# Two of a unit's four weight blocks asked for ahead of a store instead of behind it, in the first half of an MLP

## The reference, cut to what matters

```python
h = layer_norm(ALPHA * x + mix, ln1_g, ln1_b)                    # h: 576 x 2048
f = jnp.einsum('btf,fd->btd',
      jnp.square(jax.nn.relu(jnp.einsum('btd,df->btf', h, w_mlp1))), w_mlp2)   # w_mlp1: 2048 x 8192
y = layer_norm(ALPHA * h + f, ln2_g, ln2_b)
```

## Time and profile before

| | |
|---|---|
| median of 3 runs | 2890.78 us (2887.44 to 2892.32) |
| the profiled execution | 2880.25 us, its span 2878.5 us |
| PE, DVE, ACT busy | 92%, 68%, 36% of the span |
| stores of the loop | 30, at 1334.5 to 2068.9 us |
| mean granted TensorE clock | 0.963 of full speed |

### The profile page before, as it was taken

How to read it: one execution, slowest core, us unless ns; L and a number is a source line. 1 busy time by engine, 2 the same in 40 slices (tenths; PEclk the granted TensorE clock), 3 DMA queues, 4 the chain that set the end, 5 groups by cost and what they waited for, 6 DMA issues and landing times.

```text
span 2878.5 us, 52028 instructions
## 1 busy us (share of the span) xinstructions
PE 2651.6 (92%) x20033; PEld 2507.7 (87%) x20033; DVE 1950.1 (68%) x3064; ACT 1047.5 (36%) x1311; POOL 52.1 (2%) x106
## 2 busy tenths in 40 slices
PE   8999999988888899959999999999979999999997
PEld 8999999975555589948898999898979999999995
DVE  5778722337753443388777777777768888888897
ACT  3111111126754431154444444444433333333334
POOL 0000000000001000000000000000000000000000
PEclk9999999999999889979999999999999999999998
DMA  8766533223044444314555555555596566555632
GB/s 250 225 222 229 156 74 87 75 101 139 0 162 186 181 138 137 120 67 133 159 156 174 164 169 168 161 149 174 169 325 210 170 217 186 184 186 174 196 109 75
DMA packets 470707, 457.36 MB, mean 159 GB/s; under 512 B 47740, under 2 KB 418644, under 8 KB 459830
## 3 DMA queue, kind: packets, MB, share of 16 engines
q1 hardware_dynamic: 465370, 389.02, 44.2%
q0 software_dynamic: 4608, 67.11, 6.2%
q10 hardware_dynamic: 652, 0.18, 0.0%
HBM read 367.70 MB, written 96.80 MB: 161 GB/s over the span
## 4 chain that ended last, share of the span: by engine, by line
PE 38%; DVE 14%; DMA 10%; issue 8%; SPq 4%; ACT 2%; DVEq 0%; POOL 0%; ACTq 0%; POOLq 0%
PE ps L2235 24%; DMA w_s<-in_w_mlp 8%; PE ps L1899 7%; SPq L526 4%; DVE w_sl L1537 4%; DMA sg<-in_cache_slc,idx 3%; PE ps L2041 2%; DVE w_s L1542 1%; DVE w_s L1548 1%; ACT w_sh L934 1%; PE ps L2152 1%; PE ps L2051 1%; PE ps L2117 1%; PE ps L2104 1%; DVE f_raw L1686 1%
## 5 line engine op out<-in xcount | busy, mean ns | idle before, releaser
L2235 PE MATMUL ps<-h_b,w_sh 128*128 128x288 f32 x3584 | 740.2, 303 | 89.5 <-DVE w_sl L1537 67.9
L934 ACT ACTIVATE w_sh<-w_s 128x1024 fp32r<-128x1024 f32 (+1 forms) x512 | 469.9, 947 | 798.4 <-PE ps L2235 387.2
L2235 PE MATMUL ps<-f_b,w_sh 128*128 128x288 f32 x3584 | 717.7, 296 | 17.1 <-DMA f_b<-f_scratch 10.3
L2235 PEld LDWEIGHTS ps<-h_b,w_sh 128*128 128x128 f32 x3584 | 591.0, 194 | 102.2 <-DVE w_sl L1537 78.9
L1537 DVE TENSOR_TENSOR w_sl<-w_s,w_sh 128x1024 fp32r<-128x1024 f32 (+1 forms) x512 | 551.5, 1087 | 107.0 <-ACT w_sh L934 106.7
L2235 PEld LDWEIGHTS ps<-f_b,w_sh 128*128 128x128 f32 x3584 | 577.2, 189 | 20.1 <-DMA f_b<-f_scratch 11.2
L2235 PE MATMUL ps<-h_b,w_sl 128*128 128x288 f32 x1792 | 537.5, 300 | 0.0
L2235 PE MATMUL ps<-f_b,w_sl 128*128 128x288 f32 x1792 | 528.7, 295 | 0.0
L2235 PEld LDWEIGHTS ps<-h_b,w_sl 128*128 128x128 f32 x1792 | 348.6, 195 | 0.0
L2235 PEld LDWEIGHTS ps<-f_b,w_sl 128*128 128x128 f32 x1792 | 340.5, 190 | 0.0
L738 ACT ACTIVATE w_hi<-w_raw 128x2048 fp32r<-128x2048 f32 x61 | 117.0, 1918 | 613.9 <-PE ps L1899 609.7
(11 more groups left out here) (272 smaller groups left out, 2656.8 us busy)
## 6 DMA issues: line engine op xcount, KB each, us to landing
w_s<-in_w_mlp SPq DMA_DIRECT2D x512, 256.0 KB, 4.0
f_scratch<-f_st SPq DMA_DIRECT2D x32, 2016.0 KB, 7.6
f_b<-f_scratch SPq DMA_DIRECT2D x56, 1152.0 KB, 8.1
w_raw<-in_w_in SPq DMA_DIRECT2D x90, 512.0 KB, 5.2
x_r<-x_scratch SPq DMA_DIRECT2D x16, 576.0 KB, 5.0
wb<-in_cache_win SPq DMA_DIRECT2D x8, 1024.0 KB, 10.0
w_raw<-in_w_out SPq DMA_DIRECT2D x64, 128.0 KB, 2.9
w_raw<-in_w_out SPq DMA_DIRECT2D x16, 512.0 KB, 4.3
```

Source lines behind the costliest of these rows:

```text
L934: nc.scalar.activation(w_sh[m][:, :, :], blocks, ACT.Copy).then_inc(z_h[m], 1)
L2235: last = nc.tensor.matmul(ps[:, bank, 0:TH], w[b][:, at_, cols], acts(k, x), start=(start and k == 0 and n == 0), stop=(stop and k == CK - ...
```

## The change

The loop asks for blocks 2 and 3 of unit 1 ahead of the store, and for blocks 0 and 1 behind it. The wait for `z_l[M4]`, which stood behind the store, moves ahead of it with the first two blocks.

```diff
-            def w_blocks(view, c, q, u):
-
-                for b in (2, 3, 0, 1):
+            def w_blocks(view, c, q, u, blocks=(2, 3, 0, 1)):
+
+                for b in blocks:
...
-            def up_load(q, h):
+            def up_load(q, h, blocks=(2, 3, 0, 1)):
 
                 sp.wait_ge(z_l[M4], 2 * q + h - 1)
-                w_blocks(w1_v, h, q, h)
+                w_blocks(w1_v, h, q, h, blocks)
...
             with sp.Fori(0, KP - 2) as i:
                 up_load(i + 2, 0)
+                up_load(i + 2, 1, (2, 3))
                 f_store(i)
-                up_load(i + 2, 1)
+                w_blocks(w1_v, 1, i + 2, 1, (0, 1))
```

## The result

The changed kernel takes 2902.32 us, the kernel before 2887.44 us over the runs that stood beside it (medians of 5 each). The ratio is 1.0058, with a 95% interval of 1.0036 to 1.0080: slower by 0.6%, some 17 us (the two medians differ by 14.9 us). The direction was forecast, and the time lies in the range; but the size was given as 36 us, twice what came.

What follows compares the result with a forecast made beforehand. The prediction took a ring of waits, with DVE waiting for the last weight block, as the bound; 0.61 + 0.4 + 0.2 = 1.2 us a pair, 30 times, is 36 us, so 2890.8 becomes 2927 us; 8 in 10: 2899 to 2945.

Steps and rivals of the forecast that it cites:

- The ring: In the loop, 10.7 us from `low_22` to landed blocks plus 14.6 us of DVE's queue make the whole 25.3 us pair.
- Early blocks buy nothing: At DVE's one wait for all four blocks, only the last block's landing counts; blocks 2 and 3 landing early gain nothing.
- The later start: At the head of the DMA group, nothing can be issued until `low_22` is done; costs 0.61 us a pair, nearly certain.
- The sum: Added cost on DVE's wait for blocks: 0.61 + 0.4 + 0.2 = 1.2 us a pair, between 0.61 and 1.74.
- the new climb: Blocks with nothing ahead begin late and slowly, 0.22 + 0.41 us at most; taken as 0.4 us a pair.
- the turn: Between the first two blocks and the store the DMA rate dips; taken as 0.2 us a pair, ends 0 and 0.5.
- only the start counts: Rival: slow first bytes and the change from loads to store hide; 0.3 to 0.9 us a pair, 2909 us; chance 0.17.
- the store runs faster with fewer blocks behind it: Rival: the store gives back up to 1.1 us a pair, so not slower, 2883 us; chance of faster 0.09.
- The clock: Rival: PE's longer idle time draws the low clock, a pair 2 us longer or more, 2951 us and up; chance 0.06.
- unit 0's blocks: Loads asked for after unit 0's `low_22`; they and DVE's use of them shift together, costing nothing.
- the tile f_st: Tile that the later-landing store frees for ACT; needed only in the next pair, with 6 us or more of cover.
- The forecast of 11.8 us: Sign in the changed trace: first block's issue to last one's landing takes 11.8 us in place of 10.6.

Runs made afterwards that it cites:

- two counters: Changed kernel's order, but `sum_1` waits only for blocks 2 and 3, and `sum_23` for blocks 0 and 1; ratio to the kernel before 0.9983.
- the store in last place: Against the kernel before, all four blocks of unit 1 are asked for ahead of the store; 2791.7 us, ratio 0.9659.
- the kernel in which the store waits: Order of the kernel before, store then all four blocks, but the store is held until `low_22` is done; ratio to the kernel before 1.0054.
- one ahead: Changed kernel's lines with block 2 ahead of the store and blocks 3, 0 and 1 behind it; ratio to the kernel before 1.0045.
- three ahead: Changed kernel's lines with blocks 2, 3 and 0 ahead of the store and block 1 behind it; ratio to the kernel before 1.0021.
- half of the blocks asked for late: Against the kernel before: store first, then blocks 2 and 3, then a wait before blocks 0 and 1; ratio 0.9995.

## Why the prediction came out as it did

*The ring.* Right, link by link. DVE's part stayed at 14.61 us on average, the pair grew by what DVE's wait for the last block grew by, 0.58 us, and two counters and the store in last place moved the time as the ring says.

*Early blocks buy nothing.* Right: 0.71 us came back only when `sum_1` got a counter of its own.

*The later start, 0.61 us.* Right: 0.60 us when done alone.

*The sum, 1.2 us a pair.* Wrong, and this is the step that failed: "The bytes ahead of it are the same", from which I let the store and the blocks keep their durations and added only costs. By the table the recorded durations came to 1.79 + 5.56 + 1.73 = 9.08 us of each engine, where the kernel in which the store waits has 6.11 + 3.86 = 9.97: 0.89 us less, 0.55 of it in the store and 0.34 in the loads, of which four in a row fall to 290 GB/s after the second and two in a row do not.

That isn't 0.89 us of time given back, because durations can overlap. The stretch itself, averaged over 29 pairs, shows the balance:

```
                 first issue to  first byte to  last byte to  sum
                 first byte      last byte      DVE's start   us
store waits      0.87            9.68           0.59          11.14
one ahead        1.04            9.38           0.55          10.97
changed kernel   1.04            9.66           0.42          11.12
three ahead      1.04            9.36           0.36          10.76
```

The durations of the kernel in which the store waits, 9.97 us, lie in 9.68 us, so some of them do overlap; the changed kernel's 9.08 us lie in 9.66 us. So the first bytes came 0.17 us later, where the sum had 0.22; the new climb and the turn were paid for inside the stretch, which kept its length because the store and the loads took less; and the wait behind the last byte, which the sum left out, became 0.17 us shorter, for a reason that is not shown. In place of the 0.4 + 0.2 us of the sum, these terms came to -0.02 us. How much the climb and the turn cost by themselves isn't shown, only that what was given back is as large. The dip that I feared between load and store didn't come.

*The rival "only the start counts"* gave the right number (0.3 to 0.9 us a pair, 18 us in the middle; measured 0.58 and 17), but not its reason: the climb was there and was outweighed, by a store and loads that took 0.89 us less of each engine. That the balance came out at zero is luck, as it did not with one or three blocks ahead. The formula with a fixed part and bytes over a rate ("DMA: Bandwidth & Descriptors", "Anatomy of one DMA", in the Trainium skill) gives that same 18 us, and by it the experiments with 0, 1, 2 and 3 ahead would all take 25.9 us; three ahead took 25.54, so it is right by chance here.

*The rival "the store runs faster with fewer blocks behind it"* had the right effect, though only in part the right reason: a store with fewer blocks behind it is shorter, but not because fewer issues are held up (half of the blocks asked for late), and loads ahead of it shorten it too. I talked myself out of it with one row. In the earlier trace rows a store with one load behind had the same ragged end as one with four, and I concluded that loads behind don't slow it. One load behind is enough: that store took 5.79 us, against 4.87 with none. The comparison needed a store with none behind, which the loop of before doesn't have. The size that I gave it, 1.1 us at most, is near what the last places gave: 6.10 against 4.82 to 4.93. One of the signs of being wrong was that the store's bytes run clearly faster than now, and it came: 5.56 us of each engine in place of 6.10.

*The clock* stayed near 0.96 (0.963 before, 0.960 after), *unit 0's blocks* and *the tile f_st* gave no wait, as costed. The forecast of 11.8 us from first issue to last landing came out as 1610.98 - 1600.01 = 10.97 us in the pair shown, and about 11.1 on average. PE's wait for DVE's low parts grew to 67.9 us and not to 93.

## What to carry to other kernels

When a wait is for the last of several transfers, look at what stands ahead of the last one in the queue, and put anything that nobody waits for behind all of them: moving two blocks ahead of the store cost 0.6%, moving all four won 3.4%. Holding the first DMA of a busy queue back by a wait cost that wait in full here, 0.60 of 0.61 us in every turn of the ring. And don't take durations of DMAs as fixed when their neighbours change: if two transfers meet in one queue, look for the same transfer with nothing next to it before pricing an exchange of places.

## What the runs showed of the hardware

- A store of 2016 KB with nothing queued behind it took 4.87 us of each DMA engine and landed after 6.2 us. One 256 KB load and three of 8 KB queued behind it made that 5.57 and 7.0 us, four of 256 KB made it 6.10 and 7.6. Nearly all of the difference lies in the last two of each engine's eight pieces, by order of start: 1.0 and 1.3 us in place of 0.6.
- Asking for the loads 5.1 us after the store's issue, rather than 0.6 us after it, made them land earlier, and the kernel 0.3% faster (ratio 0.9957 to 0.9980).
- Four 256 KB loads of 512-byte pieces in a row behind a store ran at some 340 GB/s for the first two and 290 for the last two; two in a row stayed at 340. With nothing ahead the group dipped to 205 GB/s in the middle and went on at 233 to 333.
- With PE never idle in the loop, its granted clock there was 1.00, where with 2 us of idle time a pair it was 0.97.
